# Norms in two chains, rotary partners by DMA, and single weight parts as fillers in the trunk attentions of a two-block transformer kernel

## The reference

```python
# block b1: two layers, then a final norm
h = rms_norm(x, gain)
proj = einsum('bsd,de->bse', h, w_in)          # q, k, v, g of three branches, index heads, gates
oa = moba_attention(rope_partial(qa), rope_partial(ka), va) * silu(ga)
ob = dsa_attention(rope_partial(qb), rope_partial(kb), vb, qi, ki, wi) * silu(gb)
oc = forgetting_attention(qc, kc, vc, log_f) * silu(gc)
x = x + (sum_n gates_n * (o_n @ w_branch_n)) @ w_out
# block b2 (the trunk): two layers on 256 latent and 256 context tokens
mod = silu(cond) @ mod_w + mod_b               # nine modulations
x = x + 0.5 * g * swiglu(modulate(rms_norm(x)))                    # ffn1
x = x + m * mixer(modulate(rms_norm(x)))       # layer 0: latent attention + convolution; layer 1: grouped + neighbourhood
x = x + 0.5 * g * swiglu(modulate(rms_norm(x)))                    # ffn2
```

## Time and profile before

| what | value |
|---|---|
| median of 3 runs | 2556.89 us (2554.72 to 2557.12) |
| profiled execution | 2558.64 us, its span 2556.6 us |
| mean granted clock of TensorE | 0.992 of full |
| instructions | 39956 |
| memory traffic | 350.80 MB read, 138 GB/s over the span |

### The profile page before, as it was taken

One profiled execution on the slowest core, in us unless ns is written; L12 is line 12 of the kernel. 1 busy time (PEld: TensorE's weight loads), 2 busy tenths in 40 slices (PEclk: granted clock), 3 DMA queues, 4 the chain that ended last, 5 costly groups with the idle time before them and its releaser, 6 DMA issues.

```text
span 2556.6 us, 39956 instructions
## 1 busy us (share of the span) xinstructions
PE 2482.7 (97%) x16524; PEld 2088.3 (82%) x16524; DVE 1308.6 (51%) x1978; ACT 985.7 (39%) x1482; POOL 45.2 (2%) x71
## 2 busy tenths in 40 slices
PE   8999999999999999999989999999999999989999
PEld 7998899998978888876457888887888887857999
DVE  5478775488753433345663443333433333355654
ACT  5346544366452222252373421224321224355432
POOL 0000000000000000000030000000000000011000
PEclk9999999999999999999999999999999999999999
DMA  6447545454442322334723222234232232633553
GB/s 246 164 149 249 181 165 198 141 182 161 150 167 85 123 83 80 109 116 154 277 102 132 99 92 101 90 112 149 94 112 88 84 122 87 199 141 107 190 191 107
DMA packets 65393, 356.49 MB, mean 139 GB/s; under 512 B 14928, under 2 KB 20176, under 8 KB 29008
## 3 DMA queue, kind: packets, MB, share of 16 engines
q1 hardware_dynamic: 65232, 354.20, 39.5%
HBM read 350.80 MB, written 1.05 MB: 138 GB/s over the span
## 4 chain that ended last, share of the span: by engine, by line
PE 91%; DVE 3%; DMA 2%; ACT 2%; issue 1%; SPq 0%; POOL 0%; DVEq 0%; ACTq 0%; POOLq 0%
PE psum L1269 16%; PE psum L1270 16%; PE psum L1271 16%; PE psum L794 11%; PE psum L831 7%; PE psum L833 6%; PE psum L832 6%; PE psum L906 1%; PE psum L912 1%; PE psum L907 1%; PE psum L1158 1%; DMA wring<-in_w_mod 1%; PE psum L937 1%; PE psum L939 1%; PE psum L938 1%
## 5 line engine op out<-in xcount | busy, mean ns | idle before, releaser
L1269 PE MATMUL psum<-h_hi,w_hi 128*128 128x512 f32 (+1 forms) x1408 | 513.5, 365 | 7.3 <-DVE h_lo L2216 5.9
L1271 PE MATMUL psum<-h_hi,w_lo 128*128 128x512 f32 (+1 forms) x1408 | 511.8, 363 | 0.0
L1270 PE MATMUL psum<-h_lo,w_hi 128*128 128x512 f32 (+1 forms) x1408 | 511.7, 363 | 0.0
L1834 ACT ACTIVATE w_hi<-wring 128x1024 fp32r<-128x1024 f32 (+1 forms) x240 | 273.2, 1143 | 525.8 <-PE psum L1271 518.5
L2392 DVE TENSOR_TENSOR w_lo<-wring,w_hi 128x1024 fp32r<-128x1024 f32 (+1 forms) x240 | 318.6, 1330 | 304.7 <-ACT w_hi L1834 304.3
L831 PE MATMUL psum<-h_hi,w_hi 128*128 128x256 f32 (+1 forms) x1176 | 357.4, 304 | 1.7 <-DVE ring_lo L2247 0.9
L833 PE MATMUL psum<-h_hi,ring_lo 128*128 128x256 f32 (+1 forms) x1176 | 348.7, 297 | 0.0
L832 PE MATMUL psum<-h_lo,w_hi 128*128 128x256 f32 (+1 forms) x1176 | 348.1, 296 | 0.0
L2247 DVE TENSOR_TENSOR ring_lo<-wring,w_hi 128x1024 fp32r<-128x1024 f32 x208 | 246.7, 1222 | 162.9 <-ACT w_hi L1712 161.0
L1269 PEld LDWEIGHTS psum<-h_hi,w_hi 128*128 128x128 f32 x1408 | 266.9, 190 | 52.5 <-issue 7.2
L1271 PEld LDWEIGHTS psum<-h_hi,w_lo 128*128 128x128 f32 x1408 | 266.8, 190 | 41.5
(11 more groups left out here) (202 smaller groups left out, 3319.3 us busy)
## 6 DMA issues: line engine op xcount, KB each, us to landing
wring<-in_w_b_ffn_in SPq DMA_DIRECT2D x80, 1024.0 KB, 4.9
wring<-in_w_mod SPq DMA_DIRECT2D x72, 1024.0 KB, 5.1
wring<-in_w_b_ffn_out SPq DMA_DIRECT2D x64, 704.0 KB, 4.0
wring<-in_w_b_merge SPq DMA_DIRECT2D x24, 1024.0 KB, 4.9
wring<-in_w_b_out SPq DMA_DIRECT2D x16, 1024.0 KB, 5.0
wring<-in_w_b_in SPq DMA_DIRECT2D x16, 1024.0 KB, 6.5
wring<-in_w_b_q SPq DMA_DIRECT2D x12, 1024.0 KB, 4.9
wring<-in_w_b_k SPq DMA_DIRECT2D x12, 1024.0 KB, 4.8
```

Source lines behind the costliest of these rows:

```text
L1269: nc.tensor.matmul(acc, wh[:, k, :], rhs_hi[k], start=(k == 0), stop=False)
L1270: nc.tensor.matmul(acc, wh[:, k, :], rhs_lo[k], start=False, stop=False)
L1271: return nc.tensor.matmul(acc, wl[:, k, :], rhs_hi[k], start=False, stop=(k == n - 1))
L1834: A(part_piece(w_hi, q, i), raw_piece(c, i), ACT.Copy).then_inc(weights_rounded, 1)
```

## The change

- `CHAIN` replaces `EARLY_MODS`. The last step of every norm over 512 tokens is done in two halves of 256 tokens: squares, sums (in two banks), root, reciprocal, spreading and scaling. Modulations in a norm are cut in two halves of four matmuls each and put between those steps; what is left of them comes inside the first product (`late_mods`).
- `modulate` writes `h_hi` directly from the scaled tile and then makes the plain tile in place for `h_lo`; before, it made the plain tile and copied. The first product does two passes with `h_hi` and the third with `h_lo` (`first_passes`).
- The sums of the context and the joint sums use all four column groups.
- The sixteen rotary matmuls of the branches go. Behind chunk m + 4 of each branch SP issues four transfers of 8 partitions by 512 elements from the copied tile into a buffer `partner`; DVE multiplies there. The signs move into the table of sines.
- b2.0.att and b2.1.att: the four weight pieces come one by one, behind the reciprocal; the layer norm of the convolution takes its root straight from the bank and its gates come two units and more sooner; the exponential's table is loaded before the attention; one modulation moves from b2.1.heads to b2.1.att.

```diff
+CHAIN = {"b2.0.n1": (1, 0, 2, 0, 3), "b1.1": (1, 0, 1, 0, 2), "b2.1.n2": (1, 0, 1, 0, 2), "b2.0.nm": (1, 1, 1, 1, 0), "b2.1.nm": (1, 1, 1, 1, 0)}
+SECOND_AT = {"b2.1.n1": 3, "b2.1.n2": 1}
...
-        for at, kind in ((1, "mean"), (2, "center"), (3, "square"), (4, "var"), (5, "root"), (6, "invert"), (7, "scale")):
+        for at, kind in ((0, "mean"), (1, "center"), (2, "square"), (3, "var"), (4, "invert"), (5, "scale")):
             out[at].append((kind, 0, 0))
-        for i in range(4):
-            out[8 + i].append(("tanh", 0, i))
-            out[9 + i].append(("gate", 0, i))
-        for at, c in ((6, 0), (8, 1)):
-            out[at].append(("split", 0, c))
+        for i, at in enumerate((6, 6, 7, 8)):
+            out[at].append(("tanh", 0, i))
+        for i, at in enumerate((7, 7, 8, 9)):
+            out[at].append(("gate", 0, i))
+        for piece, at in enumerate((5, 6, 7, 8)):
+            out[at].append(("part", 0, piece))
...
-        for at, c in ((6, 0), (8, 1)):
-            out[at].append(("split", 1, c))
+        for piece, at in enumerate((4, 5, 7, 8)):
+            out[at].append(("part", 1, piece))
...
+                if c in ROTARY_AT:
+                    l, m = ROTARY_AT[c]
+                    copied_label, _, view = rotary_tile(l, m)
+                    if E.new(copied_label):
+                        sp.wait_ge(*E.at(copied_label))
...
+                    for b in (0, 8, HD, HD + 8):
+                        other = b + 8 if b % HD == 0 else b - 8
+                        sp.dma_start(partner[b:b + 8, m % 2, :], view[other:other + 8, :]).then_inc(s_partner[m % 2], 16)
...
+                norm_mods(chain[0])
+                for h in range(halves):
+                    last_sums(nm, h)
+                    norm_mods(chain[1 + h] if halves == 2 else chain[2])
+                for h in range(halves):
+                    if E.new(f"{nm}.root.{h}"):
+                        pe.wait_ge(*E.at(f"{nm}.root.{h}"))
+                    spread_half(f"{nm}.rs.{h}", banks[h], rs, h, SEQ // GROUPS * h)
+                    norm_mods(chain[3 + h] if halves == 2 else chain[4])
...
-                            if br < 2 and part in "vg":
-                                i = 2 * (part == "g") + j
-                                if l == 0 and (br, i) == (0, 0):
-                                    pe.wait_ge(s_const, 16)
-                                rotate_bank(br, i)
...
+                        A(h_hi[:, k, half_of(g)], squares[:, k % 4, half_of(g)], ACT.Identity, scale=mscale[:, k, g:g + 1],
+                          bias=mods[:, l, 24 * which + k, g:g + 1]).then_inc(shifted, 1)
...
+                both(0)
+                both(1)
+                plain_first()
+                low(0)
+                low(1)
+                both(2)
+                ahead(2)
+                both(3)
+                low(2)
+                ahead(3)
+                for k in range(4, KD):
+                    both(k)
+                    low(k - 1)
+                low(KD - 1)
...
+                for n in range(16):
+                    if n < 14:
+                        split_chunk(flow[n + 2])
...
+                    if 2 <= n % 8 < 6:
+                        rope_tile(4 * (n // 8) + n % 8 - 2)
```

More of the change, by code:

```diff
@@ new lines, in norm_banks @@
+            def norm_banks(nm, sums):
+                after = nm.replace(".n", ".ffn")
+                if after in FFNS:
+                    first = [(piece_number(after, 0) + i) % BANKS for i in (0, 1, 2, 3, 7)]
+                else:
+                    rotating = 7 if nm in ("b2.0.nm", "b2.1.nm") else state["rotating"]
+                    first = [state["bank"] % rotating]
+                    while len(first) < PARTS * NORM_N[nm] // BANK:
+                        first.append((first[-1] + 1) % rotating)
+                free = [b for b in range(BANKS) if b not in first and b not in sums] + [b for b in sums if b not in first]
+                return free[0:3]
@@ L994, in norm @@
-                acc = take(f"{nm}.rs", fixed=(bank + 5) % BANKS)
-                if E.new(f"{nm}.root"):
-                    pe.wait_ge(*E.at(f"{nm}.root"))
-                for j in range(GROUPS):
-                    row = C("ident")[:, GW * j:GW * j + 1].broadcast_to([P, P])
-                    mm = product(acc[:, per * j:per * j + per], row, rs[:, 0:per], 0, 1)
-                mm.then_inc(summed, 1)
-                E.step(summed, f"{nm}.rs")
-                norm_mods(nm, middle, None)
+                state["rows_bank"], *banks = norm_banks(nm, [book.banks[f"{nm}.sum.{h}"] for h in range(halves)])
@@ L1004, in hold @@
             def hold(nm):
+                state["todo"] = [(m, a) for m in MODS.get(nm, []) for a in range(2)]
                 if nm == "b1.1":
@@ L1233, in modulation @@
                 per = KD // GROUPS
-                for a in range(per):
+                for a in some:
                     for j in range(GROUPS):
@@ L2154, in bank, with norm @@
                 return psum[:, E.bank(label), 0:N]
-            def norm(nm, gain=None, to=None, ahead=None):
+            def norm(nm, gain=None, ahead=None, l=None, which=None):
                 N = NORM_N[nm]
@@ L2168, in norm @@
                         ahead(i)
-                if E.new(f"{nm}.rs"):
-                    dve.wait_ge(*E.at(f"{nm}.rs"))
-                scaled(nm, gain, to, ahead)
+                if gain is not None:
+                    scaled_plain(nm, gain, ahead)
+                else:
+                    scaled(nm, ahead, l, which)
             def joint_norm(nm, ahead):
@@ L2176, in joint_norm @@
                     ahead(i)
+                per = SEQ // GROUPS
+                if E.new("context.sum'"):
+                    dve.wait_ge(*E.at("context.sum'"))
+                V.reciprocal(rs[:, per:2 * per], rs[:, per:2 * per]).then_inc(normed, 1)
+                E.step(normed, "context.root")
                 if E.new("joint.c7"):
```

414 lines of the change are left out of this document (250 added, 164 removed).

## The result

The changed kernel takes 2566.55 us (median of 6 runs, 2563.56 to 2568.96) where the kernel before takes 2557.01 (6 runs): ratio 1.0037, 95% interval 1.0026 to 1.0048. It is 9.5 us slower. The forecast was 2527 and faster; the result lies outside the range too.

What follows compares the result with a forecast made beforehand. PE was taken as the bound, busy 2482.7 of 2556.6 us. Rotary 14.2, sums 2.4, norms 3.2, attentions 5.5 and 2.5, clock 2 made 29.8 us off 2558.64, so median 2527 us; range 2513 to 2541.

Steps and rivals of the forecast that it cites:

- rotary matmuls: Branches: sixteen 512-column matmuls leave PE's queue at 0.89 us each, 14.2 us gained; SP's added transfers costed at nothing.
- sums and norms: Sums with all column groups gain 2.4 us; norms gain 3.2 us in all, b2.0.n2 itself 0.
- b2.1.att: Second trunk attention: early table 1.3 us, single pieces behind the reciprocal 3.7 net, moved modulation 0.5; sum 5.5 us gained.
- b2.0.att: First trunk attention: two PE waits mostly go, 2 us of new waits in units 7 and 8; net 2.5 us gained.
- clock: Shorter waits save about half a stretch at the lower clock level: 2 us, between 7 gained and 4 lost.
- Where a chunk was late the new order of chunks helps: Norms: 0.5 us gained each for b2.0.nm, b2.1.nm, b2.1.n1 and the joint norm; ACT waited 1.22 us in b2.0.nm.
- (b): Branches: SP's queue takes back 9 of the 14.2 us rotary gain, 2536 us; chance 0.12.
- (d): Branches: SP's queue delays rotary partners, PE stops at each of 16 tiles; 2575 us at 3 us a tile; chance 0.03.
- Rival (e): Branches: rotary matmuls only hid something else and the chunk pace stays 6.54 us; 2541 us; chance 0.03.
- Rival (a): Waits close more fully: norms give 9, attentions 8 and 6, clock 7; 2510 us; chance 0.12.

Runs made afterwards that it cites:

- e5_att: e3_both with the first piece of b2.1.out rounded in unit 5, not 4, and b2.0.att's gates one to a unit: 2539.49 us, ratio 0.9923.
- e3_both: The changed kernel with bias transfers one weight chunk sooner and three, not two, modulation chunks before each b2.x.in's two projection chunks: 2543.43 us, ratio 0.9961.
- e12_no_early_table: e9_att20_before without the early exponential in b2.1.heads, so its table loads at the first unit of b2.1.att: 2534.93 us, ratio 0.9911.
- e9_att20_before: e5_att with b2.0.att alone as before the change (convolution's norm, gates from unit 9, weight chunk halves together in units 6 and 8): 2532.47 us, ratio 0.9902.

## Why the prediction was wrong, point by point

| term | forecast | measured (medians; ratios) |
|---|---|---|
| rotary matmuls | 14.2 gained | 10.2; 13.0 gained |
| sums and norms | 5.6 gained | 5.0; 4.4 gained |
| b2.1.att | 5.5 gained | 8.8; 7.7 gained, once its first piece is in unit 5 |
| b2.0.att | 2.5 gained | 7.0; 5.4 lost, even with one gate to a unit |
| the two misplaced edits in the attentions | 0 | 3.9; 9.7 lost |
| plan of the weights, ring and bias | 0 (inside the 3.2 us of the norms a gain of 0.5 for each of four) | 23.1; 19.4 lost |
| clock | 2 gained | no term of its own: it follows the waits |

With the medians 10.2 + 5.0 + 8.8 - 7.0 - 3.9 - 23.1 = -10.0, with the ratios 13.0 + 4.4 + 7.7 - 5.4 - 9.7 - 19.4 = -9.4, for a measured loss of 9.5. Most of this sum closes because each run stands on the one before; what it tests is that rotary, norms and attentions add: 10.2 + 5.0 + 1.8 = 17.0 us, where e5_att, which has all three, is 17.7 faster than the kernel before.

**The step that failed** is the sentence "Where a chunk was late the new order of chunks helps". It looked at the wait of 1.22 us in the earlier trace rows and gave half a microsecond to the chunk that now comes sooner. It did not ask which slot of the ring the next chunk takes, nor walk SP's queue past the moved segment. The rule was on hand: a chunk goes out when the chunk four places before it is used. With the old plan the third projection chunk replaces a modulation; with the new one it replaces the first projection chunk. The same step missed that a number in SP's code counts within a segment of the plan, so that a change of the segments' lengths moves 32 transfers that no line of the diff touches. The gain that the sentence counted on needed no such swap: in e3_both the second projection chunk goes out one place sooner than before and not two, 1.2 us after the first modulation (1079.52, 1078.29) where it was 2.2 (1098.88, 1096.67), and ACT does not wait for it. The runs showed a loss of 23.1 us by the medians, 19.4 by the ratios, where the sum had a gain of about 2.

**Rotary matmuls: right in mechanism, oversized.** The term measured 10.2 to 13.0 us for 14.2. DVE splits at 43.80, 49.43 and 55.05 us in the changed kernel, 5.6 us apart with a rotary step behind each, where it was 6.54. SP takes 2.64 us for the four transfers, as costed, and nothing waits for the partners. So the two rivals on SP's queue in the branches, (b) and (d), had the right queue in the wrong place. Rival (e) is out.

DVE's timeline of the changed kernel:

```profile
43.80 2.36 DVE L2394 TENSOR_TENSOR ring_lo<-wring,w_hi 128x1024 fp32r<-128x1024 f32 x2 [1.34 <-ACT w_hi L1798]
...
49.43 2.36 DVE L2394 TENSOR_TENSOR ring_lo<-wring,w_hi 128x1024 fp32r<-128x1024 f32 x2 [1.21 <-ACT w_hi L1798]
```

The section "Rules for kernel authors" of the Trainium skill's page "DMA: Bandwidth & Descriptors" spoke against 64 small transfers. In the branches its price did not reach PE. It did where nobody had costed it: the 32 bias transfers hold SP 0.72 us each (23.05 / 32), and a megabyte of weights stood behind them.

**Norms: right in sum, wrong in a step.** I had PE start 2.3 us sooner after the spread and give it all back. PE starts 1387.21 - 1383.27 = 3.94 us after the first spread, 4.80 before: 0.9 sooner, since a product needs `h_hi` of both halves, and ACT gets to the second only at 1386.47, behind the second spread. I had timed the first. From the spread of b2.0.n2 to that of b2.1.n1 it is 370.70 us for 371.47: 0.8 gained where I had 0. The sum for all norms, 5.0 or 4.4 for 5.6, is measured only as a whole; that it comes so near, although PE's start was put 1.4 us too early and this norm's gain 0.8 us too low, is partly luck. ACT's four results of a tile took 2.25 us (1096.44 to 1098.69 in b2.0.nm), not 2.46. PE and ACT in b2.0.n2, then ACT in b2.0.nm:

```profile
1383.27 1.10 PE L831 MATMUL psum<-rs,cst 128*128 128x64 f32 x8 [0.20 <-DVE rs L2260]
...
1386.47 1.83 ACT L1820 ACTIVATE h_hi<-squares,mods,mscale 128x256 fp32r<-128x256 f32 x3 [0.92 <-DVE squares L2336]
...
1387.21 0.47 PE L1371 MATMUL psum<-h_hi,w_hi 128*128 128x512 f32 x1 [0.67 <-ACT h_hi L1820]
...
1096.44 1.10 ACT L1820 ACTIVATE h_hi<-squares,mods,mscale 128x256 fp32r<-128x256 f32 x2
...
1098.69 1.09 ACT L1820 ACTIVATE h_hi<-squares,mods,mscale 128x256 fp32r<-128x256 f32 x2
```

**b2.1.att: right, and undersized.** The table, the single pieces behind the reciprocal and the moved modulation give 8 us and not 5.5. The table's own part came out at 2.5 by the medians with 1.3 forecast, too near the scatter to choose. The exponential starts at 2241.40, when the load of 1.28 begun at 2240.10 has just ended (e12_no_early_table). The Trainium skill's page "ScalarE: Activation LUTs", section "What ACT_TABLE_LOAD costs", adds a drain of 1.38 us to the load; no run here shows it. What I missed is the landing of the first chunk: I checked that DVE had 1.2 us to spare in each unit, and not that the piece had arrived by unit 4: its transfer leaves at 2267.91, when the modulation of unit 2 has been used, and ACT wants it at 2273.7 (2277.13 - 3.44). Four modulation chunks had gone out in the 6 us before it, the transfers of this stretch moved 6.29 MB in 20 us, and a landing that takes 4.8 us elsewhere took 9.

**b2.0.att: wrong in sign.** I saw "8.5 and 6.8 us against 5 to 6 of PE" on DVE in units 7 and 8 and charged 2 us. The waits themselves were 2.7 to 3.0 us. What I did not charge is the clock around them, 5.0 us more in e5_att's profile than in e9_att20_before's, and what I did not weigh is that DVE had room for the gates where they were, from unit 9 on.

**Clock.** I had given 2 us for shorter waits. It is no term on its own: in the changed kernel the windows around the new waits stand at 0.83, and where e3_both removes the waits they stand at 1.00. So a wait costs more than its length: 10.5 us of wait and 3.1 of clock in the work behind it are 13.6, and taking the wait away gave 12.6 by the medians and 13.6 by the ratios. Of the lower clock only what falls on work is paid. At the joint norm the clock is lower without a longer wait, and that part is open.

**The best version** is e9_att20_before, the change with four repairs (bias one chunk sooner, three modulations before the projection's chunks, b2.1.att's pieces from unit 5, b2.0.att as before): 2532.47 us, ratio 0.9902 (0.9886 to 0.9917), 1.0% faster than the kernel before and 34 us faster than the changed one. It lies in the range that was given for the whole change, which says little for the sum: one part of the change is taken out in it, and the terms differ. Rival (a) stood outside that range with its own figure (2510, range from 2513), not only with its far end.

## What to carry to other kernels

When chunks of a ring change places, list for each chunk near the change the one whose slot it takes and when that is used; a swap of two entries can tie a chunk to a product that has not run. Search the code for everything that counts along the moved list: a transfer tied to "the fifth chunk of this segment" moves without a line of diff. Ahead of an engine's critical step put only work whose input has surely arrived, and after a loss, repair single numbers before you give up the idea: 27 of the 34 us lay in a handful of them, the other 7 in a part that was better left as it had been. When two times differ by 3 us with overlapping intervals, compare the stage that was edited in the two profiles, and a stage that was not.

## What was not expected of the hardware

A wait on PE cost 1.2 to 1.4 times its length: the one of 10.53 us was worth 12.6 to 13.6 us, the one of 9.97 us made the kernel 14.1 us slower (by its interval 8 to 20), as the granted clock fell from 2.4 to 1.2 GHz during the wait and was still low for part of the 7 us behind it. A spreading matmul with half the columns took nearly the same time: eight records with 64 columns 1.10 us, eight with 128 columns 1.13. The stretch after the joint norm is at 0.74 of full in the changed kernel with hardly any idle time in it, where the kernel before has longer waits and 0.91; one attempt to move work there did not change it, and its cause stays open.
